# Late gate projections computed as seven products of half blocks, with their weight sums on GpSimd between the steps of the last DRAM sum sets

## What is computed

```
xn    = rms_norm(x)
proj  = xn @ w_in                       # q, k, v of mixers A and B
att_a, att_b = the two chunked attentions           # 512 x 1024 each
y_a, y_b = att_a @ w_branch_a, att_b @ w_branch_b   # 512 x 2048 each
gates = sigmoid(xn @ w_gate)            # 512 x 4096
merged = gates[:, :2048] * y_a + gates[:, 2048:] * y_b
h = x + merged @ w_out
h = h + square(relu(rms_norm(h) @ w_mlp_in)) @ w_mlp_out
out = rms_norm(h)
```

## Time and profile before

| | |
|---|---|
| median of 3 runs | 2479.97 us (2479.5 to 2480.07) |
| span of the profiled execution | 2477.4 us |
| TensorE busy | 2460.5 us, 99% |
| DVE busy | 1660.1 us, 67% |
| ACT busy | 1062.9 us, 43% |
| POOL busy | 193.0 us, 8% |
| DMA engines | 517.11 MB, mean 209 GB/s |

### The profile page before, as it was taken

The page is one execution under the profiler, slowest core; times in us unless marked ns, Lnnn a source line. Parts: engine busy times, 40 slices in busy tenths (PEclk is TensorE's granted clock), DMA queues, the critical chain, the costliest instruction groups (busy, mean ns, idle before and its releaser), DMA issues.

```text
span 2477.4 us, 34658 instructions
## 1 busy us (share of the span) xinstructions
PE 2460.5 (99%) x14162; PEld 2176.6 (88%) x14162; DVE 1660.1 (67%) x2260; ACT 1062.9 (43%) x1382; POOL 193.0 (8%) x185
## 2 busy tenths in 40 slices
PE   9999999999999999999999999999999999999998
PEld 8898898898888888888999999999998888888886
DVE  6566555556333332544788888888869788877898
ACT  5566755556222222312433433333335444444445
POOL 0011000100010100101200000000001011110010
PEclk9999999999999999999999999999999999999999
DMA  7788998888898999965554434433479666566652
GB/s 262 212 254 240 237 250 244 234 251 224 231 263 246 245 251 254 257 181 151 167 191 153 135 131 131 134 128 130 135 230 336 229 230 225 190 225 232 233 191 108
DMA packets 226819, 517.11 MB, mean 209 GB/s; under 512 B 30672, under 2 KB 159840, under 8 KB 215152
## 3 DMA queue, kind: packets, MB, share of 16 engines
q1 hardware_dynamic: 213712, 363.52, 44.1%
q0 software_dynamic: 12672, 151.00, 24.3%
q10 hardware_dynamic: 288, 0.54, 0.1%
HBM read 489.80 MB, written 176.20 MB: 269 GB/s over the span
## 4 chain that ended last, share of the span: by engine, by line
PE 95%; DVE 3%; ACT 1%; issue 1%; DMA 0%; SPq 0%; ACTq 0%; DVEq 0%
PE bank L1728 31%; PE bank L1730 30%; PE bank L1729 30%; PE bank L1803 1%; PE bank L1838 1%; PE bank L1817 1%; DVE ring L1519 0%; DMA stream<-in_x_features 0%; DVE up_lo L1411 0%; DVE form_lo_b L1377 0%; DVE stream L1547 0%; DVE stream L1568 0%; DVE at_lo L1261 0%; ACT q_twice L752 0%; DVE stream L1559 0%
## 5 line engine op out<-in xcount | busy, mean ns | idle before, releaser
L1045 DVE TENSOR_TENSOR w_lo<-landing,w_hi 128x1024 fp32r<-128x1024 f32 x199 | 247.7, 1244 | 447.4 <-ACT w_hi L696 447.3
L1728 PE MATMUL bank<-xn_hi,w_hi 128*128 128x512 f32 x1184 | 464.7, 392 | 2.3 <-DVE w_lo L1202 1.3
L1730 PE MATMUL bank<-xn_hi,w_lo 128*128 128x512 f32 x1184 | 461.2, 390 | 0.0
L1729 PE MATMUL bank<-xn_lo,w_hi 128*128 128x512 f32 x1184 | 460.7, 389 | 0.0
L696 ACT ACTIVATE w_hi<-landing 128x1024 fp32r<-128x1024 f32 x199 | 210.9, 1060 | 575.6 <-PE bank L1730 575.2
L919 ACT ACTIVATE up_hi<-up_raw 128x1792 fp32r<-128x1792 f32 x128 | 218.1, 1704 | 401.8 <-PE bank L1730 391.5
L968 ACT ACTIVATE ring<-down_raw 128x1024 fp32r<-128x1024 f32 x224 | 237.5, 1061 | 312.4 <-PE bank L1730 312.4
L1519 DVE TENSOR_TENSOR ring<-down_raw,ring 128x1024 fp32r<-128x1024 f32 x224 | 285.4, 1284 | 68.2 <-ACT ring L968 68.0
L1411 DVE TENSOR_TENSOR up_lo<-up_raw,up_hi 128x1792 fp32r<-128x1792 f32 x128 | 259.9, 2030 | 85.2 <-ACT up_hi L919 85.2
L1728 PEld LDWEIGHTS bank<-xn_hi,w_hi 128*128 128x128 f32 x1184 | 222.4, 188 | 47.3 <-issue 3.3
L1730 PEld LDWEIGHTS bank<-xn_hi,w_lo 128*128 128x128 f32 x1184 | 222.2, 188 | 46.9
(11 more groups left out here) (192 smaller groups left out, 4386.4 us busy)
## 6 DMA issues: line engine op xcount, KB each, us to landing
down_totals<-in_down_blocks POOLq DMA_DIRECT2D x64, 1024.0 KB, 9.4
up_raw<-in_up_units SPq DMA_DIRECT2D x128, 512.0 KB, 3.4
down_raw<-down_totals SPq DMA_DIRECT2D x128, 512.0 KB, 4.4
down_raw<-in_down_blocks SPq DMA_DIRECT2D x96, 512.0 KB, 4.3
landing<-in_w_in SPq DMA_DIRECT2D x71, 512.0 KB, 6.2
landing<-in_w_gate SPq DMA_DIRECT2D x64, 512.0 KB, 6.3
landing<-in_w_out SPq DMA_DIRECT2D x32, 512.0 KB, 3.7
hidden_rows<-hidden_out SPq DMA_DIRECT2D x32, 512.0 KB, 3.4
```

The lines of the kernel that those rows point to most:

```text
L1045: nc.vector.tensor_tensor(w_lo[:, s, :], landing[:, u % LAND, :], w_hi[:, s, :].bitcast(F32), ALU.subtract).then_inc(unit_lo, 1)
L1728: nc.tensor.matmul(dst, a_hi, b_hi, start=start, stop=False, **kw)
L1729: nc.tensor.matmul(dst, a_hi, b_lo, start=False, stop=False, **kw)
L1730: return nc.tensor.matmul(dst, a_lo, b_hi, start=False, stop=stop, **kw)
```

## The change

The two stages "branches and gates in turn" become two stages one after the other. First come all 32 branch units (`branch(w)`), a before b. The y of the blocks 2 to 7 are kept: y_a in place of the attention's outputs (`keep_branch`), y_b stored to DRAM (`store_yb`) and loaded again (`load_yb`). Then come the 48 gate units as 12 groups of four (`gate_unit`), each 42 matmuls with 256 columns, in the order `GATE_ORDER`. The normed x is made again in its seven forms (`x_form_block`, `x_form_sums`, `x_form_high`, `x_form_low`). The raw gate weights come from a host-side rearrangement `gate_units`, 512 KB a unit, into three places. DVE makes the lo part of the seven forms (`gate_low`) and puts the products together (`mixed_gate`, `fourth_gate`); ACT makes the hi part (`gate_high`) and the sigmoid (`open_gate`).

The weight sums of every gate unit are made by POOL (`gate_sums`). The first 12 of the 18 sum sets keep their starts. The last 6 sets, 36 parts, are issued between the gate sums of the 48 units, three parts in four units.

```diff
+KEPT = 2
+GROUPS = 2 * (D // CB - KEPT)
+GATE_UNITS = 4 * GROUPS
+GATE_ORDER = (list(IN_TURN) + [(s, v) for s in range(2, GROUPS - 2) for v in range(4)]
+              + [(GROUPS - 2 + s, v) for s, v in IN_TURN])
+LATE_SETS = 12
...
+            def load_gate(n):
+
+                s, v = GATE_ORDER[n]
+                if n == 0:
+                    sp.wait_ge(att_ready, HEADS)
+                elif n < 3:
+                    sp.wait_ge(unit_lo, UNITS1 + BRANCH_UNITS - 4 + 2 * n)
+                else:
+                    sp.wait_ge(gate_lo_done, n - 2)
+                sp.dma_start(gate_raw[n % 3][:, 0:4, :].rearrange("p b n -> p (b n)"),
+                             gate_units[s % 2 * (D // CB) + KEPT + s // 2, v]).then_inc(gate_landed[n % 3], 16)
...
+            load_gate(1)
+            load_gate(2)
+            load_x_forms(2)
+            for n in range(3, GATE_UNITS):
+                load_gate(n)
+                if n in (3, 4, 5):
+                    store_yb(n + 2)
...
+            def gate_high(n):
+
+                act.wait_ge(gate_summed, 3 * n + 3)
+                if n == 0:
+                    act.wait_ge(merged, KEPT)
+                elif n == 1:
+                    act.wait_ge(unit_used, UNITS1 + BRANCH_UNITS)
+                else:
+                    act.wait_ge(gate_used, n - 1)
+                nc.scalar.activation(gate_hi[n % 2], gate_raw[n % 3][:, 1:8, :], ACT.Copy).then_inc(gate_hi_done, 1)
...
+            def gate_low(n):
+
+                dve.wait_ge(gate_hi_done, n + 1)
+                nc.vector.tensor_tensor(gate_lo[n % 2], gate_raw[n % 3][:, 1:8, :], gate_hi[n % 2].bitcast(F32),
+                                        ALU.subtract).then_inc(gate_lo_done, 1)
...
-            for m in range(2 + STEPS):
+            def gate_sums(n):
+
+                pool.wait_ge(gate_landed[n % 3], 16 * (n // 3) + 16)
+                raw = gate_raw[n % 3]
+                add(raw[:, 4:6, :], raw[:, 1:4:2, :], raw[:, 0:1, :].broadcast_to([P, 2, CB])).then_inc(gate_summed, 1)
+                pool.wait_ge(gate_summed, 3 * n + 1)
+                add(raw[:, 6, :], raw[:, 4, :], raw[:, 3, :]).then_inc(gate_summed, 1)
+                pool.wait_ge(gate_summed, 3 * n + 2)
+                add(raw[:, 7, :], raw[:, 6, :], raw[:, 2, :]).then_inc(gate_summed, 1)
+
+            for m in range(LATE_SETS):
                 pool.wait_ge(unit_used, 12 + 8 * m if m < 10 else 84 + 10 * (m - 9))
                 for part in range(6):
                     totals(m, part)
+            parts = 6 * (2 + STEPS - LATE_SETS)
+            for n in range(GATE_UNITS):
+                gate_sums(n)
+                for k in range(parts * n // GATE_UNITS, parts * (n + 1) // GATE_UNITS):
+                    totals(LATE_SETS + k // 6, k % 6)
             form_sums()
...
+            def gate_unit(n, s, v):
+
+                pe.wait_ge(gate_lo_done, n + 1)
+                if v == 0 and s == 0:
+                    pe.wait_ge(att_ready, HEADS)
+                elif v == 0 and s == 1:
+                    pe.wait_ge(yb_kept, 6)
+                elif v == 0:
+                    pe.wait_ge(gate_mixed, 5 * (s - 1))
...
+            for w in range(BRANCH_UNITS):
+                branch(w)
+            for n, (s, v) in enumerate(GATE_ORDER):
+                gate_unit(n, s, v)
```

More of the change, by code:

```diff
@@ L41 @@
 UP_END = len(IN_TURN)
+KEPT = 2
[4 more added lines that the diff above has]
+LATE_SETS = 12
+X_BATCHES = (range(0, 4), range(4, 6), range(6, 8))
 UP_FORM = (0, 3, 5, 1, 4, 2, 6)
@@ L92, in up_place, with gate_end, x_batch @@
     return UP_ORDER.index((s, v))
+def gate_end(s):
+    return GATE_ORDER.index((s, 3))
+def x_batch(kp):
+    return next(b for b, kps in enumerate(X_BATCHES) if kp in kps)
 def summed_in_dram(n):
@@ L575, in _, with load_x_forms @@
-            for j in range(2):
-                load_branches(B2_END + j, NBR - 2 + j)
+            def load_x_forms(batch):
+                kps = X_BATCHES[batch]
+                sp.wait_ge(unit_used, UNITS1 + (0, BRANCH_UNITS // 2, BRANCH_UNITS)[batch])
+                for kp in kps:
+                    for i in (kp, kp + KP):
+                        slots = slice(0, 8, 7) if i < KP else slice(3, 7, 3)
+                        sp.dma_start(x_raw[kp][:, slots, :], x_blocks[:, i, :].rearrange("p (h n) -> p h n", h=2))\
+                            .then_inc(x_form_landed[batch], 16)
@@ new lines, in _ @@
+            act.wait_ge(at_lo_done, KB // 2)
+            for w in range(2, BRANCH_UNITS):
+                split(B2 + w // 4, w % 4)
+                if w >= 3 and w % 2 == 1:
+                    keep_branch((w - 3) // 2)
+                if 12 <= w < 16:
+                    x_form_high(w - 12)
+                elif w in (26, 27):
+                    x_form_high(w - 22)
+            for n in range(GATE_UNITS):
+                gate_high(n)
+                if n == 1:
+                    keep_branch(15)
+                elif n in (2, 3):
+                    x_form_high(n + 4)
+                if n >= 4 and GATE_ORDER[n - 4][1] == 3:
+                    open_gate(GATE_ORDER[n - 4][0])
+                if n >= 2 and GATE_ORDER[n - 2][1] == 3:
+                    gate_first_product(GATE_ORDER[n - 2][0])
@@ L879, in merged_part @@
                     .then_inc(merged_hi, 1)
+            act.wait_ge(gate_used, GATE_UNITS - 4)
             merged_part(0)
-            split(B2_END, 2)
             merged_part(1)
-            split(B2_END, 3)
+            split(B3, 0)
             merged_part(2)
-            for u in range(4):
-                split(B2_END + 1, u)
-                merged_part(3 + u)
+            merged_part(3)
+            open_gate(GROUPS - 2)
+            gate_first_product(GROUPS - 1)
+            split(B3, 1)
+            merged_part(4)
+            merged_part(5)
+            open_gate(GROUPS - 1)
+            split(B3, 2)
+            merged_part(6)
             def form_high(kp):
@@ new lines, in x_form_block @@
+            def x_form_block(kp):
+                batch = x_batch(kp)
+                dve.wait_ge(x_form_landed[batch], 16 * 2 * len(X_BATCHES[batch]))
+                for i in (kp, kp + KP):
+                    slots = slice(0, 8, 7) if i < KP else slice(3, 7, 3)
+                    nc.vector.scalar_tensor_tensor(
+                        out=x_raw[kp][:, slots, :], in0=x_raw[kp][:, slots, :], scalar=gains[:, 0, i:i + 1],
+                        in1=rms_row[:].rearrange("p (h n) -> p h n", h=2), op0=ALU.mult, op1=ALU.mult)\
+                        .then_inc(x_form_raw, 1)
@@ new lines, in _ @@
+            for w in range(2, BRANCH_UNITS):
+                split(B2 + w // 4, w % 4)
+                if w in (3, 5):
+                    scaled_a((w - 3) // 2)
+                elif w in (19, 21):
+                    merge_b((w - 19) // 2)
+                if 8 <= w < 12:
+                    x_form_block(w - 8)
+                elif w == 12:
+                    x_form_sums(0)
+                elif 13 <= w < 17:
+                    x_form_low(w - 13)
+                elif w in (24, 25):
+                    x_form_block(w - 20)
+                elif w == 26:
+                    x_form_sums(1)
+                elif w in (27, 28):
+                    x_form_low(w - 23)
@@ new lines, in _ @@
+            for n in range(GATE_UNITS):
+                gate_low(n)
+                if n == 1:
+                    x_form_block(6)
+                    x_form_block(7)
+                    x_form_sums(2)
+                elif n in (3, 4):
+                    x_form_low(n + 3)
+                if n >= 4 and GATE_ORDER[n - 4][1] == 3:
+                    through_gate(GATE_ORDER[n - 4][0])
+                if n >= 2 and GATE_ORDER[n - 2][1] == 3:
+                    mixed_gate(GATE_ORDER[n - 2][0])
+                if n >= 3 and GATE_ORDER[n - 3][1] == 3:
+                    fourth_gate(GATE_ORDER[n - 3][0])
```

386 lines of the change are left out of this document (250 added, 136 removed).

## The result

The changed kernel takes **2587.43 us** (2585.89 to 2589.2, 4 runs), the kernel before beside it 2479.73 us (2478.96 to 2480.07, 4 runs): a ratio of **1.0436, 95% interval 1.0421 to 1.0451**. It is slower by 107.7 us where 56 were forecast and 98 was the upper end of the range. The direction and the mechanism were right, the size was not.

What follows compares the result with a forecast made beforehand. TensorE, busy 99%, bounds the kernel before; afterwards POOL's queue paces the gate stage: -7 + 270 + 40.5 + 12.3 = 315.8 us for 261.1, plus 1 at the branch start, span 2533.1, median 2536 us; range 2498 to 2578.

Steps and rivals of the forecast that it cites:

- POOL's queue sets the pace: Gate stage: sets plus additions cost POOL 54.0 us per eight units, TensorE needs 40.3; 2499 to 2571 us, chance 78%.
- two thirds of TensorE's wait: Gate stage: two thirds of TensorE's stall for `gate_lo` fall behind part 2 of each set, after a 14.5 us wait.
- If all else is hidden, the change gives 19.1 us: Gate units on TensorE: 48 units take 242.0 us at 5.04 each in place of 261.1.
- the end behind the last gate unit costs nothing either: End of gate stage: last merged block's lo part comes some 14 us later, needed behind three units of 5.44 us.
- a forecast of "hidden": Rival in the gate stage: sets land sooner; below 33.3 us a set everything is hidden, 2462 us; chance 5%.
- A set takes 48.0 us in the stretch shown in full ... I take 47: POOL's late sets, first part's issue to last part's end: 43.1 to 49.8 us before the change, taken as 47.
- Behind part 2 two units' additions (7.0 us) lie beside a wait of 7.03 us, just covered: POOL's queue within each set: these additions fit inside the DMA wait and add nothing to the period.
- I take 3.5: POOL's additions for one gate unit: 3.5 us, between 2.4 undisturbed and 4.4 with one DVE lo part in the way.
- The first set then loses some 4 us: Start of gate stage: unit 5 loads only after unit 2's lo part; first set counted as begun at -7 us.
- The last set: Sixth set, end of gate stage: last addition 40.5 us after part 0, then 12.3 us through the last unit.
- The clock as a rival: Gate stage: TensorE's idle gaps lower its clock, hidden up to 2.7 slow units of eight; 2580 to 2704 us, chance 8%.
- The rule for the DMA's price: POOL's sets: 2.0 us per DMA plus bytes at 436 GB/s makes 32.2 us a set, the change wholly hidden.

Runs made afterwards that it cites:

- a_sets_in_up: Changed kernel with the last six sum sets moved out of the gate stage into the up stage; 2543.04 us, ratio 1.025.
- e_no_late_sets: Changed kernel with its six late sum sets left out, the down stage reading an earlier step's sums; 2478.78 us, ratio 0.9999.
- b_dve_sums: Changed kernel with DVE making the gate units' weight sums two units ahead, sets left on POOL in the gate stage; 2512.45 us, ratio 1.014.
- d_spare_adds: As b_dve_sums, but POOL also makes same-size additions on spare memory at the changed kernel's places for 32 units; 2540.7 us, single run.
- h_start_only: Changed kernel with the branch's last y store a load earlier and the last two x blocks made later, sets staying; 2584.14 us, ratio 1.0429.
- g_sets_around: Changed kernel with two late sets moved before the gate stage, four into the output projection, and h_start_only's start; 2548.78 us, ratio 1.0278.
- c_hidden_adds: Changed kernel with set parts moved between the gate sums so fewer additions stand uncovered, none behind part 5; 2564.98 us, ratio 1.0343.

## Why the prediction was wrong, by its own steps

*"POOL's queue sets the pace"*: shown. Without sets in the queue the excess goes (a_sets_in_up, e_no_late_sets); with the sums taken off the queue and the sets left, 78.8 of it go (b_dve_sums); with the queue kept and all that depended on it cut, POOL keeps its period (d_spare_adds). The forecast that two thirds of TensorE's wait lie behind part 2 of each set was too high: in the four full periods it is 33.8 of 63.6 us.

*"If all else is hidden, the change gives 19.1 us"*: right as arithmetic (5.04 us a unit forecast, 5.00 measured), wrong as a gain. The start, costed in with POOL's chain and otherwise at nothing, takes 11.3 us, and "the end behind the last gate unit costs nothing either" was 2.8 short, 2.2 of it two waits of TensorE for DVE's low parts of weights, 0.7 us ahead of the output projection and 1.5 in it. Even a forecast of "hidden" should have said "no change" (2462 was its figure; e_no_late_sets measured 2478.8).

*"A set takes 48.0 us in the stretch shown in full ... I take 47"*: **this term failed**. The sets are 53.3 us long, mean of the five behind the first. That is 6.3 us in each of the four full periods and most of 3.8 in the last, some 29 of the 48.4 us by which the gate stage misses its forecast (364.2 for 315.8). I read the length of a set where it stood beside the old stage and carried it over as a constant. Step by step the runs have 47.4 us before, 49.5 in the new stage with nothing between the parts (b_dve_sums), 52.9 with additions between them (d_spare_adds) and 53.3 in the changed kernel. Neither of the two steps, 2.1 and 3.4 us, is shown to be one cause. The eight sets for the down projection that start ahead of 600 us, beside the same blocks of q, k and v in both kernels, are longer in the changed kernel as well (49.3 for 46.6 us, 48.9 in b_dve_sums), so that the 2.1 need not be the new stage's traffic; and a set with no additions in it took 52.5 in d_spare_adds, started straight behind another, so that the 3.4 need not be the additions. No run separates whether loads that come in bursts hold a part's landing. How long the sets are is measured; how the 6.3 us split stays open.

*"Behind part 2 two units' additions (7.0 us) lie beside a wait of 7.03 us, just covered"*: not covered. Two costs that are equal on paper are not hidden when both vary; part 3 then goes out when the longer of the two is done, 7.4 us in the set shown, and from part 2 to part 3 it is 7.9 us where it was some 6 in b_dve_sums. It is some 2 of the 3.4.

*"I take 3.5"* for a unit's additions: 3.83 in the mean over 48 units (144 of 1277 ns). Small: behind part 5 two units' took 7.5 us for the 7.0 forecast.

*"The first set then loses some 4 us"*: **the second term that failed**, by 16 us (63.2 for 47). I followed the place of unit 5 and not SP's queue, in which unit 3 stands behind loads that wait for the branch's end, and I did not add the transfers that come due together there. h_start_only recovered 5 of the 16 in its profile; the rest was not undone, so that its cause is read from the waits and not shown.

*The last set*: 56.6 us from its first part to the end of the stage for 52.8, the same cause as the set's length. Together: 16.2 + 4 x 7.1 + 3.8 = 48.4, the whole miss of the stage. The span missed by 52.4 (108.1 for 55.7). The other 4 lie outside the stage: 2.8 behind it, as above, and some 1 ahead of it, where TensorE waits 1.8 us in the branch stage and 1 was forecast. The 2.6 us from span to median were too many as well; in the profiled run it is 1.9 (2587.35 for 2585.5).

*The clock as a rival*: it did fall, to 0.81 to 0.92 of its full level in the windows above, spells of the 1.2 GHz level behind TensorE's gaps. A period's eight units then took 43 to 47 us of TensorE's time for 40.0. But the period was 60 us by POOL's queue, so it was hidden, as the prediction had it for up to 2.7 slow units of eight. The Trainium skill, "TensorE: Matmul & The Clock Gate", section on HAM oscillation, says that such gaps drop the array to half clock; by that rule, the trace agrees.

*The rule for the DMA's price* from the Trainium skill, "DMA: Bandwidth & Descriptors", that gave 32.2 us a set: no run came near. The shortest set seen is the 43.1 us of the earlier trace rows, the longest, leaving out the first of the gate stage, 60 us (g_sets_around, beside the output projection).

## What to carry to other kernels

Work that is due soon must not stand in a queue that waits for slow transfers, however idle that engine looks: ask of each wait in that queue who stands behind it, and of each transfer what is loaded in the stretch it would move to. A background transfer's price went with the work that was loaded ahead beside it and not with the share of the DMA engines: a set cost nothing beside the down stage's twelve places (32.7 us of work) at 89% DMA share, and nothing beside the four places of the old late stage (4 x 5.44 = 21.8 us) at 91%, where TensorE never waited more than 0.2 us; beside three places (15 us) it cost some 6 us in the gate stage and 11 in the up stage. These stages differ in more than their places, and no run changed the places alone, so that this is a reading of four stages and not a shown rule. And before work is taken off TensorE, price the start of the stage: 19 us of matmuls were saved here and 11 of them were lost in the first 24.5 us, before three of the 48 units were done.

## What the runs showed of the hardware that was not expected

- A set of four copies and four accumulations in DRAM, 8.39 MB, took 47.4 us on average beside 512-column gate units, 49.5 beside 256-column ones and 56.0 beside the down stage's loads at a DMA share of 0.89. A set started straight behind another is longer at once: its second part went out 14.8 us after the first in c_hidden_adds for 10.3 in the changed kernel. What a set does to others varies far more: the median 512 KB load went from 3.6 to 6.0 us in the gate stage, from 4.4 and 4.7 to 13.1 and 12.5 in the down stage.
- Additions of POOL on memory that no other engine touches made DVE's instructions longer: a lo part took 2.28 us in the mean for 2.02, an addition of 512 elements 0.95 for 0.69. In the other direction, POOL's three additions of a unit take 2.92 us alone and up to 6.54 beside DVE (814.48 us in the changed kernel). The Trainium skill, "SBUF — State Buffer", section on who interferes with whom, says that a DVE instruction with two SBUF inputs contends with a GpSimd instruction that reads SBUF, and that issue order decides who is held; by that rule, both directions are as the trace has them; which of two was issued first was not read here.
- A stage at 0.38 DMA share with one wait of 9 us at its start had a granted clock of 0.79 in those first 24.5 us and 1.00 in every later slice. One gap at the start is paid twice, by the wait of 9.0 us and by the matmuls behind it (15.5 us for 13.2).
